# Recurrent unit of a decoder layer: decay from exponential and tanh on ScalarE without reciprocals, samples' first steps folded in, one scan per half

## What is computed

```python
r = sigmoid(xc @ wa + ba);  i = sigmoid(xc @ wx + bx)      # 16 blocks of 64 channels
log_a = -8 * r * softplus(-lam)
a = exp(log_a);  mult = sqrt(-expm1(2 * log_a))
a, mult = (0, 1) at the very first step of the prompt
b = mult * i * xc;  b[:, 0] += a[:, 0] * h0                # h0: 0 for the prompt, the state for a sample
h[t] = a[t] * h[t-1] + b[t]
out_a = (h * gelu(gate_lru)) @ w_lru_o
out_b = silu(layernorm(dwconv31(conf_a * sigmoid(conf_b)))) @ w_conf_o
merged = sigmoid(bg_lru) * out_a + sigmoid(bg_conf) * out_b
```

## Time and profile before

| | |
|---|---|
| median of 3 runs | 941.74 us (940.17 to 942.42) |
| span of the profiled execution | 937.2 us |
| PE busy / DVE busy | 865.9 us (92%) / 708.8 us (76%) |
| ACT busy / POOL busy | 414.7 us (44%) / 299.3 us (32%) |
| the recurrence and its cover (from 258 to 494 us) | PE busy 228.28 of 236.00 us |

### The profile page before, as it was taken

How to read it: one execution, slowest core, us unless ns; L and a number is a source line. 1 busy time by engine, 2 the same in 40 slices (tenths; PEclk the granted TensorE clock), 3 DMA queues, 4 the chain that set the end, 5 groups by cost and what they waited for, 6 DMA issues and landing times.

```text
span 937.2 us, 13282 instructions
## 1 busy us (share of the span) xinstructions
PE 865.9 (92%) x5477; PEld 727.1 (78%) x5477; DVE 708.8 (76%) x943; ACT 414.7 (44%) x379; POOL 299.3 (32%) x177
## 2 busy tenths in 40 slices
PE   3899999989999999989999996899999999999983
PEld 3798888989988797889994556778887878777851
DVE  3529999999795996992013567789899988988847
ACT  5443232323246223251211123477677777777623
POOL 5344555736520110143310332113232444332010
PEclk9999999999999999999999996899999999999987
DMA  9988668412120140342446114689999999999932
GB/s 317 341 232 288 228 235 286 132 47 91 45 90 2 45 135 1 101 140 91 163 148 258 46 45 186 203 320 348 350 374 340 350 344 362 365 347 346 346 113 96
DMA packets 76538, 194.41 MB, mean 207 GB/s; under 512 B 7972, under 2 KB 49060, under 8 KB 66093
## 3 DMA queue, kind: packets, MB, share of 16 engines
q1 hardware_dynamic: 71245, 182.19, 54.8%
q0 software_dynamic: 5088, 10.99, 4.4%
q10 hardware_dynamic: 144, 0.38, 0.1%
HBM read 185.41 MB, written 16.47 MB: 215 GB/s over the span
## 4 chain that ended last, share of the span: by engine, by line
PE 42%; DVE 33%; DMA 12%; ACT 5%; issue 4%; SPq 2%; POOL 1%; POOLq 0%; DVEq 0%; ACTq 0%
PE ps L1284 16%; DVE ps L1685 13%; PE ps L1272 6%; DVE slot_c L1853 6%; PE ps L1372 6%; DMA ring_a<-in_w_up 5%; PE ps L1466 5%; DMA ring_a<-in_w_gate 4%; PE ps L1489 2%; DVE slot_a L1853 2%; SPq L538 2%; ACT slot_c L1080 2%; PE ps L1316 1%; DVE region_d L1743 1%; DMA region_b<-in_w_ada 1%
## 5 line engine op out<-in xcount | busy, mean ns | idle before, releaser
L756 POOL TENSOR_TENSOR w_lo<-ring_a,w_hi 128x2048 fp32r<-128x2048 f32 x28 | 132.0, 4716 | 251.3 <-ACT w_hi L941 251.3
L1853 DVE TENSOR_TENSOR slot_c<-ring_a,slot_c 128x2048 fp32r<-128x2048 f32 x72 | 164.0, 2288 | 22.5 <-ACT slot_c L1080 22.1
L1284 PE MATMUL ps<-hm_hi,w_hi 128*128 128x272 f32 x720 | 151.8, 292 | 7.7 <-ACT region_c L980 4.0
L1080 ACT ACTIVATE slot_c<-ring_a 128x2048 fp32r<-128x2048 f32 x72 | 137.2, 1916 | 46.3 <-DMA ring_a<-in_w_gate 26.4
L1284 PE MATMUL ps<-hm_lo,w_hi 128*128 128x272 f32 x720 | 148.6, 288 | 0.0
L1284 PE MATMUL ps<-hm_hi,w_lo 128*128 128x272 f32 x720 | 148.6, 289 | 0.0
L1685 DVE SCALAR_TENSOR_TENSOR ps<-region_b,rt,ps 128x512 f32<-128x512 f32 x208 | 137.6, 744 | 0.0
L1284 PEld LDWEIGHTS ps<-hm_hi,w_hi 128*128 128x128 f32 x720 | 112.4, 189 | 22.9 <-issue 18.6
L1466 PE MATMUL ps<-slot_c,xgt_hi 128*128 128x512 f32 x384 | 126.8, 400 | 1.3 <-DVE slot_c L1853 1.3
L1284 PEld LDWEIGHTS ps<-hm_lo,w_hi 128*128 128x128 f32 x720 | 113.2, 189 | 0.0
L1284 PEld LDWEIGHTS ps<-hm_hi,w_lo 128*128 128x128 f32 x720 | 112.8, 190 | 0.0
(11 more groups left out here) (333 smaller groups left out, 1444.4 us busy)
## 6 DMA issues: line engine op xcount, KB each, us to landing
ring_a<-in_w_gate SPq DMA_DIRECT2D x32, 1024.0 KB, 7.9
ring_a<-in_w_up SPq DMA_DIRECT2D x32, 1024.0 KB, 8.5
ring_a<-in_w_down SPq DMA_DIRECT2D x32, 1024.0 KB, 7.3
ring_a<-in_w_in SPq DMA_DIRECT2D x24, 1024.0 KB, 7.1
region_c<-in_w_ada SPq DMA_DIRECT2D x20, 1024.0 KB, 5.6
ring_a<-in_w_conf_o SPq DMA_DIRECT2D x4, 1024.0 KB, 6.3
ring_a<-in_w_lru_o SPq DMA_DIRECT2D x4, 1024.0 KB, 5.1
region_d<-in_w_ada SPq DMA_DIRECT2D x3, 1024.0 KB, 12.9
```

Of the source, the lines that this page charges most:

```text
L756: g.tensor_tensor(w_lo[:, q % 2], raw[split_at[q] % 2], w_hi[:, q % 2].bitcast(F32), ALU.subtract)\
L1080: s_.activation(hi_slot(n), raw_slot(n), ACT.Copy).then_inc(unit_hi, 1)
L1284: ins = mm(ps[:, bank(n) + h, 0:HALF], w[:, q % 2, k, m * P:(m + 1) * P], x[:, k, h * HALF:(h + 1) * HALF], start=(k == 0 and w is w_hi an ...
L1853: v.tensor_tensor(lo_slot(n), raw_slot(n), hi_slot(n).bitcast(F32), ALU.subtract).then_inc(unit_lo, 1)
```

## The change

ACT computes a = exp(-8 * softplus(-lam) * r) directly into rec (the factor is a new tile sp8n) and t = tanh(sp4 * r) into tt, one after the other, when the last gate of a half has been drained. DVE computes (a + 1) * t into xc, which is 1 - a; ACT takes the root of tt in place and turns xc back into a = 1 - xc with an Identity; DVE computes (a + 1) * sqrt(t) into tt, which is mult, and sets it to 1 at step 0. Before the scan the first step of each sample gets a * h0 added to b and its a set to 0, and a at step 0 of every chunk is set to 0, so that one scan over the flat 128x2176 tile does four chunks and all samples. The scan writes rec, and hlast and z read rec. The two calls of reciprocal, the saved step 0, the eight small sample operations, `lru_1b` and `root` go away. The root is no longer at the place of ("co", h, 2) on ACT but in `decay`, right behind the tanh. In the list `work` the r/i pairs of half 1 move forward: c 0 and 1 behind ("in", G_BC + 1, 2), c 2 and 3 behind ("in", G_BC + 1, 3). The gated operations on DVE stand at other places among the parts of the recurrence.

```diff
+        xc_flat, ii_flat, rec_flat = (x[:, at:at + GC * T] for x, at in
+                                      ((region_d, 4352), (region_b, 4352 + GC * T), (region_b, 4352 + 2 * GC * T)))
+        sp8n = sb("sp8n", [P, KC])
...
-                if (h, w, m) == (1, "co", GC - 1):
-                    work += [(x, 1, c) for c in range(2) for x in ("r", "i")]
+                if (h, w) == (1, "co") and m >= 2:
+                    work += [(x, 1, c) for c in range(2 * m - 4, 2 * m - 2) for x in ("r", "i")]
             for m in range(GC):
                 work += [(w, h, m)]
-                if (h, w, m) == (1, "co", 0):
-                    work += [(x, 1, c) for c in range(2, GC) for x in ("r", "i")]
...
-            def root(g):
-
-                act.wait_ge(t_copied, g + 1)
+            def decay(g):
+
+                act.wait_ge(sp_ok, 1)
+                if g:
+                    act.wait_ge(z_ok, g)
+                for c in range(GC):
+                    s_.activation(rec[:, c, :], tt[:, c, :], ACT.Exp, scale=sp8n[:, g * GC + c:g * GC + c + 1])
+                for c in range(GC):
+                    ins = s_.activation(tt[:, c, :], tt[:, c, :], ACT.Tanh, scale=sp4[:, g * GC + c:g * GC + c + 1])
+                ins.then_inc(t_ok, 1)
+                act.wait_ge(fall_ok, g + 1)
                 s_.activation(tt, tt, ACT.Sqrt).then_inc(sqrt_ok, 1)
+                s_.activation(xc, xc, ACT.Identity, bias=ones[:, 0:1], scale=-1.0).then_inc(decay_ok, 1)
...
-                    if work[n] in (("co", 0, 2), ("co", 1, 2)):
-                        root(work[n][1])
...
-                    g = int(kind == "i")
-                    act.wait_ge(sp_ok, 1)
                     act.wait_ge(pair_act, sum(by_act[:n + 1]))
-                    for c in range(GC):
-                        ins = s_.activation(tt[:, c, :], tt[:, c, :], ACT.Tanh,
-                                            scale=sp4[:, g * GC + c:g * GC + c + 1])
-                    ins.then_inc(t_ok, 1)
+                    decay(int(kind == "i"))
...
+            ch.link(v.tensor_scalar(sp8n[:, :], acc, -8.0, None, ALU.mult))
...
-                ch.do(v.tensor_tensor(ii, ii, xc, ALU.mult))
+                ch.link(v.tensor_tensor(ii, ii, xc, ALU.mult))
                 dve.wait_ge(t_ok, g + 1)
-                ch.link(v.tensor_scalar(rec, tt, 1.0, None, ALU.add))
-                ch.link(v.reciprocal(rec[:, 0:2], rec[:, 0:2]))
-
-            def lru_1b(g):
-
-                v.reciprocal(rec[:, 2:GC], rec[:, 2:GC]).then_inc(t_copied, 1)
-                dve.wait_ge(t_copied, g + 1)
+                v.scalar_tensor_tensor(xc, rec, 1.0, tt, ALU.add, ALU.mult).then_inc(fall_ok, 1)
 
             def lru_2(g):
 
-                ch.link(v.tensor_copy(hst[:, 0, 0:GC], ii[:, :, 0]))
                 dve.wait_ge(sqrt_ok, g + 1)
-                ch.link(v.scalar_tensor_tensor(tt, tt, 2.0, rec, ALU.mult, ALU.mult))
+                ch.link(v.scalar_tensor_tensor(tt, rec, 1.0, tt, ALU.add, ALU.mult))
+                ch.link(v.memset(tt[:, :, 0:1], 1.0))
+
+            def lru_3(g):
+
                 ch.link(v.tensor_tensor(ii, ii, tt, ALU.mult))
-
-            def lru_3(g):
-
-                ch.do(v.tensor_scalar(rec, rec, 2.0, -1.0, ALU.mult, ALU.add))
-                ch.link(v.tensor_copy(ii[:, :, 0], hst[:, 0, 0:GC]))
-                for m in range(GC):
-                    ch.do(v.tensor_tensor_scan(xc[:, m, 0:TP], rec[:, m, 0:TP], ii[:, m, 0:TP], 0.0, ALU.mult, ALU.add))
+                dve.wait_ge(decay_ok, g + 1)
+                before = hst[:, 0, :].rearrange("p (m s) -> p m s", m=GC)
+                ch.link(v.tensor_tensor(before, first_step(xc), rt[:, g * GC:(g + 1) * GC, R_H0:R_H0 + NS], ALU.mult))
+                ch.do(v.tensor_tensor(first_step(ii), first_step(ii), before, ALU.add))
+                ch.do(v.memset(first_step(xc), 0.0))
+                ch.link(v.memset(xc[:, :, 0:1], 0.0))
+                ch.link(v.tensor_tensor_scan(rec_flat, xc_flat, ii_flat, 0.0, ALU.mult, ALU.add))
...
             lru_1(0)
             gated("co", 0, 0)
-            lru_1b(0)
+            lru_2(0)
             gated("co", 0, 1)
+            lru_3(0)
             gated("co", 0, 2)
-            lru_2(0)
+            lru_4(0)
             gated("co", 0, 3)
-            lru_3(0)
-            lru_4(0)
             dve.wait_ge(z_ok, 1)
             for k in range(GC, KC):
                 lru_conv(k)
             last_rows(1, 35, 1)
+            lru_1(1)
             gated("co", 1, 0)
-            lru_1(1)
+            lru_2(1)
             gated("co", 1, 1)
-            lru_1b(1)
+            lru_3(1)
             gated("co", 1, 2)
+            lru_4(1)
             gated("co", 1, 3)
-            lru_2(1)
-            lru_3(1)
-            lru_4(1)
```

More of the change, by code:

```diff
@@ L327, in build @@
         t_ok = sem("t_ok")
-        t_copied = sem("t_copied")
+        fall_ok = sem("fall_ok")
         sqrt_ok = sem("sqrt_ok")
+        decay_ok = sem("decay_ok")
         z_ok = sem("z_ok")
@@ L1713, in lru_conv, with first_step @@
                 ins.then_inc(xc_ok, 1)
+            def first_step(x):
+                return x[:, :, TP:].rearrange("p m (s t) -> p m s t", s=NS)[:, :, :, 0]
             def lru_1(g):
@@ L1745, in lru_4 @@
-            def lru_4(g):
[L1747 to L1755, removed]
+                dve.wait_ge(decay_ok, g + 1)
@@ new lines, in lru_3 @@
+                before = hst[:, 0, :].rearrange("p (m s) -> p m s", m=GC)
[4 more added lines that the diff above has]
+                ch.link(v.tensor_tensor_scan(rec_flat, xc_flat, ii_flat, 0.0, ALU.mult, ALU.add))
+            def lru_4(g):
+                ch.do(v.tensor_copy(hlast[:, g * GC:(g + 1) * GC, :], rec[:, :, TP - 1:]))
@@ L1758, in lru_4 @@
                 zz = z[:, g * GC:(g + 1) * GC, :]
-                v.tensor_tensor(zz, zz, xc, ALU.mult).then_inc(z_ok, 1)
+                v.tensor_tensor(zz, zz, rec, ALU.mult).then_inc(z_ok, 1)
             def last_rows(i, n, bank_rows):
```

## The result

| | before | after |
|---|---|---|
| median of 7 runs each | 941.74 us (939.4 to 944.41) | 936.07 us (934.84 to 938.5) |
| ratio | | 0.9936, 95% interval 0.9913 to 0.9960 |
| span of the profiled execution | 937.2 us | 935.9 us |

The two spans differ by 1.3 us only. In the new runs the time of an execution is its span and 1.8 to 2.0 us more. So the profiled execution of before took about 939 us, under all seven times of its kernel, and that of after (937.7) was one of the two longest of its seven. Spans must not be subtracted here; stages can.

The account below looks back on a forecast made before the run. PE was taken to bound the kernel (228.28 of 236.00 us busy in the recurrence's stretch). Terms -1.27 +1.3 -2.65 -0.65 = -3.3, and +0.2, gave 941.7 - 3.1 = 938.6 us; range 936.9 to 941.5.

Parts of the forecast that it names:

- the one hidden drain: Half 0, PE idle at 313.7: the view says issue, but DVE drains co 0 late behind a reciprocal; 1.3 us.
- One load ahead of the exponential: ACT, half 0: one table load of 1.28 us before Exp, within bounds of 0 to 2.6 us.
- t_ok: ACT, half 0: exponentials and tanh finished at 309.6, against 305.8 before.
- Scan first, split behind it: Half 0, DVE and POOL: scan due at 320.5, split at 320.76; scan runs to 325.6, split to 330.1.
- wait for w_lo: PE, start of half 1: begins at 330.2 behind the delayed split, giving back 1.3 us; net 0 there.
- z_ok: DVE, half 1: product into z done at 393.4, 20 us earlier than 416.7.
- The 2.65 us gap: PE idle ahead of lo 0, behind DVE's recurrence and an ACT drain; claimed to go, worth 2.65 us.
- three waits: PE's waits as read from the view: 2.7 us on an ACT drain, 1.3 "issue", 0.9 on POOL's w_lo.
- the split first: Rival, 0.27: half 0's scan waits for POOL's split, delaying co 2's drain; total -2.3 to -1.6, 939.9 us.
- The allowance of 0.2 for new waits between semaphores: Term of the sum: 0.2 us added for small new waits, putting lo 0 at 416.4.
- so the shift is kept: Behind 419.5: PE runs without a gap to 492.5 and later loads follow, so the whole 3.1 us gain stays.
- the best case: Rival, 0.10: Exp needs no load, half 0's scan starts at 319.2, 1.3 us stay saved; -4.3, 937.4 us.

Follow-up runs that it names:

- filling the gap: Kernel before with 22 small products that nobody reads put on PE into the idle time ahead of lo 0; ratio to before 1.0004 (0.9977 to 1.0032).
- the run with the pad: Changed kernel with 38 small products that nobody reads put on PE ahead of lo 0; mean 939.5 us, ratio to before 0.9980.
- the late scan: Changed kernel with six small fills on DVE ahead of the flat scan of half 0, so POOL's split is first; mean 937.9 us, ratio to before 0.9952.
- drain first: Kernel before with the drains of co 0 and co 1 of half 0 each moved ahead of its reciprocal; mean 939.7 us, ratio to before 0.9991.
- idle gap: Changed kernel with five unread copies on ACT ahead of the drain of in BL 2, so PE idles before lo 0; mean 943.8 us, ratio to before 1.0032.
- old list: Changed kernel with PE's list as before and half 1's drain of co 0 ahead of the recurrence's first part; mean 944.6 us, ratio to before 1.0015.
- list only: Kernel before with only PE's list changed, r/i of half 1 behind in 2 and in 3; mean 944.8 us, ratio to before 1.0048.
- after, third: Changed kernel without edit, timed a third time on another chip; mean 934.8 us, ratio to before 0.9911 (0.9878 to 0.9944).

## Why the prediction was right or wrong

**Right, by its own steps.** The chain of waits and the one hidden drain named what could be gained, and only that came back. One load ahead of the exponential, none ahead of the tanh, the load of the root hidden: t_ok at 309.7, forecast 309.6. The exponential started 1.29 us after its load began (303.17 to 304.46). The Trainium skill ("ScalarE: Activation LUTs", What ACT_TABLE_LOAD costs) gives 2.66 us for a switch; this trace does not agree. Scan first, split behind it, the 1.3 us of the drain given back as a wait for w_lo (forecast 330.2, was 329.67). r/i of half 1 did not wait. z_ok at 391.7, forecast 393.4. The 2.65 us gap is closed and nothing took its place. The split of half 1 was lengthened by 1.1 us (5.60) and not by 2, at no cost. The text named three waits; the view has a fourth, of 1.2 us at 270, which stands before the stretch that the change touches and is the same in both kernels. Two further points of the text were made real by experiments: the split first (1.1 us, forecast 0.8 to 1.5), and the list's dependence on DVE. That the scan was first was forecast by 0.3 us and measured at 0.24 to 0.33, in three traces of three; the margin is thin, but it was worked out.

**Wrong: the sum, by 0.9 us.** Lo 0 was forecast at 416.4 and came at 415.46. The scan was priced at 5.05 from four scans of 512 at 1.14 and "the start of one"; it took 4.69, whereby the split ended at 329.6 and not 330.1, and PE resumed 0.5 us before its forecast. The allowance of 0.2 for new waits between semaphores had nothing to pay. And a gap was priced at the idle time in its row: start to start the two that closed at 313.7 and 322.6 gave 1.8 us and not 1.27, of which the wait for w_lo took 1.6 back, and the one ahead of lo 0 gave 2.8 and not 2.65. These are mis-sized terms; the mechanism held, and alone they would have left the time within the range (937.7).

**Wrong: "so the shift is kept".** This step priced PE's idle time at its length. The runs show that an idle time can also cost what follows: 1.5 us behind it in two of the four traces with a gap of 2.65 ahead of lo 0, 2.3 behind one of 4.1, and half clock behind one of 5.1. In the execution that the prediction read this did not happen, and its clock row said 1.00; the second kind of price was never asked for, though the same trace shows half clock behind the idle time of 4.0 us at 209.7.

**Wrong: the range.** Its lower end added "half a us of scatter" to the best case. The stage of the experts alone spans 290.4 to 297.6 us in fourteen traces of kernels that do the same there, and a comparison of the kernel before with itself came out at 1.0016. The range reached only 1.7 us below the forecast, while single executions of the kernel before have a standard deviation of 2.7 us. The 4.5 us that the text found between span and median come from the same scatter: 1.8 to 2.0 are constant in the new runs, and the rest is that the profiled execution was a short one of its kernel.

**Open** is about 1 us. The pooled times say 6.2 with a standard error of 0.5, the pieces 4.1 to 5.6. It may be that the clock falls behind the old gap in more executions than the two of four seen, or chance; filling the gap was to tell, and its interval of 5 us was too wide. The recorded mean of the granted clock over whole executions leans to the first: 0.9721 in 96 executions of the kernel before, 0.9741 in the 12 with the gap filled, 0.9746 in the 22 of the changed kernel, where one loss of 1.5 us in 937 is worth 0.0016; but the run with the pad, which has no such gap, stands at 0.9722. A part may also lie behind w_out: the pad cost 3.6 us where its trace shows 2.3, the late scan 3.1 for 1.1, each with a standard error of 1.0 to 1.2. No run here decides it.

## What to carry to other kernels

Ask of every cheaper operation which idle time of the bounding engine it ends: 31 us less work on DVE moved what follows by 4 us, and by nothing that shows without the reorder of PE's list. Price an idle time of TensorE of some us at more than its length, as its clock may be down when it resumes, and do not trust one trace to show it. Where a long instruction of DVE and one of POOL hold each other up, as the scan and the split here, put what others wait for ahead of them in DVE's queue; with the drain ahead of the scan, the scan waited for the split and held up nobody.

## What was not expected of the hardware

- The granted clock fell to its lower level behind idle times of PE of 2.64 (one trace of the kernel before), 2.7 (drain first), 4.1 (idle gap) and 5.1 us (old list); for 3.2 to 6.0 us products then started every 0.23 us instead of 0.125. Behind the same 2.7 in two other traces it did not, nor behind 2.3 us in the run with the late scan. Behind the 1.2 us at 329.7 (three traces of the changed kernel) it never did. The length alone does not tell: it also fell behind 1.8 us at 256.5 (idle gap) and behind 1.9 to 2.0 us at 176.5 in three traces (list only; after, third; scan late), with a granted clock of 0.60 in 176 to 180 in the first of these.
- A flat scan of 2176 columns takes 4.69 us, 2.16 ns a column, against 1.19 us for one of 512 (2.33 ns). Beside a split that began first it takes 8.05 to 8.23.
- A copy of 128x132 behind the scan was held up by POOL's split in both halves: 3.72 us, against 0.22 in the run with the late scan.
